# Weighing values before scoring keys in each decode slot of a hybrid decoder step

## The chip, the core and the metric

The kernel runs on one core of one Trainium2 chip. The metric is device time in microseconds (us), the median of several executions; lower is better. One execution is also recorded by the hardware profiler, and all rows below come from that one.

## What is computed

One inference step of a one-layer decoder: a prompt of 16 + 512 tokens and 8 running sequences with 4 new tokens each. The part that matters here is the stick-breaking attention of the running sequences over 4096 cached positions, whose keys and values lie in pages of 128 positions in device memory:

```python
p = x @ w_in                                    # one projection, 53 column blocks of 128
k_past = cache_k[l][page_table].reshape(bs, past, H_ATT, HEAD_DIM)
v_past = cache_v[l][page_table].reshape(bs, past, H_ATT, HEAD_DIM)
z = einsum('bqhd,bkhd->bhqk', q, k) * SB_SCALE + bias
log_keep = where(mask, log_sigmoid(-z), 0.0)
log_pass = cumsum(log_keep, axis=3, reverse=True) - log_keep
a = where(mask, exp(log_sigmoid(z) + log_pass), 0.0)
h_att = einsum('bhqk,bkhd->bqhd', a, v)
```

Beside it stand prompt attention, a short convolution, an mLSTM, an output projection and an MLP. Everything is float32.

## The kernel before

The program has five phases in a row: the input projection together with the decode attention over the cache (`phase_project`), the mixing groups, the output projection, the MLP, and the end. The change is in the first alone.

`phase_project` is laid out by hand in numbered **slots**. Every engine runs its own loop over the same slots k = -16 ... 72, and semaphores tie the loops together. In a slot TensorE multiplies one or two **chunks** of the projection (`chunk`, lines 430 to 432: 16 groups of three matmuls each, about 6.1 us a chunk). Slots 0 to 63 also take one eighth of the cache of one sequence each, in two steps that lie nine slots apart (`LAG = NSTEP + 1 = 9`):

- `scores(k)` (L463) multiplies the transposed keys `kT` of step k with the queries, into `S`. It waits for `kt_done`, VectorE's transpose of the keys (L676). There is one `kT`, so the transpose for step k+1 waits until `scores(k)` is done. GpSimd's gather of the keys for step n (L397, 2 MB, two buffers) waits for the transposes up to step n-2. 
- `weigh(k - 9)` (L478) multiplies the attention weights `aT` of the older step with its values, into `O`. It has two halves. Each half m waits for its own 1 MB of values (`v_in`), which SyncE loads in two transfers (`load_v`, L294) as soon as the value buffer is free; `value_slot` gives three buffers in turn, so the values of half m wait for half m-3 (`av_done`). Hence the second half of a slot gets its values issued after the first half of the slot before, and the first half of a slot after the second half of the slot but one before.

Slots 0 to 8 have `scores` alone, 64 to 72 `weigh` alone, and the 55 slots from 9 to 63 both. Of these 55, 20 have two chunks ("long" slots, some 16 us) and the others one ("short", some 10 us).

SyncE's loop is one queue in order: in slot k it first issues the weight chunks of w_in (`load_w`, L282), each after VectorE's `low` of three chunks earlier (`lo_done`, L669), and then the values that `weigh` of the slot frees. VectorE's loop in slot k does `low` of the chunks of slot k+1, every eighth slot the stick-breaking scan (`stick`), and then the transpose of the keys of step k+1. ScalarE splits the weights (`high`, L547) and empties PSUM (`evac`, L565), in the order first `high` of slot k+1, `evac` of the units that end in slot k, second `high`. At the head of slots 9, 17, ... 65 TensorE turns the weights (`turn`, L491), and one slot later the outputs (`turn_output`, L499).

Of the kernel before, what the change touches and what calls it, by code (L numbers as in the profile page):

```python
# [105 lines left out]
LAG = NSTEP + 1  # L106
# [14 lines left out]
def chunks_of(k):  # L121

    return range(max(0, first_chunk(k)), min(NCHUNK, first_chunk(k + 1)))
# [12 lines left out]
def value_slot(m):  # L136

    return m % VR if m < LAST else (VR, VR + 1, 1, 2, 0)[(m - LAST) % (VR + EXTRA)]
# [7 lines left out]
def value_fill(m):  # L146

    return 1 + sum(value_slot(n) == value_slot(m) for n in range(m))
# [13 lines left out]
def phase_project(nc, dram, keep):  # L162
# [12 lines left out]
    with ExitStack() as ctx:  # L175
# [27 lines left out]
        def value(m, q):  # L203

            slot = value_slot(m)
            return v_nat[:, 2 * slot + q, :] if slot < VR else v_last[:, 2 * (slot - VR) + q, :]
# [196 lines left out]
        def _(pe):  # L403
# [31 lines left out]
            def chunk(n):  # L435

                pe.wait_ge(lo_done, n + 1)
                if gate_chunk(n):
                    g = n - QCHUNK
                    if g == 0:  # L440
                        pe.wait_ge(evac_done, HA - 1)
                    product_of(n, 0, 8, P, 8 * g, g == 0, g == 1).then_inc(chunk_done, 1)
                else:
                    p, part = pair_and_part(n)
                    for j in range(2):
                        if part == 0 and p > 0:
                            pe.wait_ge(evac_done, place(U_GATE) + 1 if 2 * p == HA else place(2 * (p - 1) + j) + 1)
                        last = product_of(n, j, CK, 2 * P, CK * part, part == 0, part == 3)
                        if part == 3 and j == 0:
                            last.then_inc(unit0_done, 1)  # L450
                    last.then_inc(chunk_done, 1)

            def scores(k):
                b, s = divmod(k, NSTEP)
                pe.wait_ge(kt_done, k + 1)
                if s == 0:
                    pe.wait_ge(q_done, b + 1)
                if s % 4 == 0 and b > 0:
                    pe.wait_ge(p_done, 2 * b - 1 + s // 4)
                for g in range(2):  # L460
                    for db in range(4):
                        for j in range(NJ):
                            last = mm(S[32 * j:32 * (j + 1), s // 4, (s % 4) * P:(s % 4 + 1) * P], qd[:, j, g, db, :],  # L463
                                      kT[:, :, 2 * j + g, db, :], start=(g == 0 and db == 0), stop=(g == 1 and db == 3))
                last.then_inc(qk_done, 1)

            def weigh(k):
                b, s = divmod(k, NSTEP)
                if s == 0 and b > 0:
                    pe.wait_ge(o_copied, b)  # L470
                pe.wait_ge(aT_done, 2 * b + 1 + s // 4)
                for half in range(2):
                    m = 2 * k + half
                    pe.wait_ge(v_in[value_slot(m)], 32 * value_fill(m))
                    for q in range(2):
                        quarter = 2 * half + q
                        for j in range(NJ):
                            last = mm(O[32 * j:32 * j + 2 * NQ, 0:2 * HD], aT[:, s, j, quarter, :],  # L478
                                      value(m, q)[:, 2 * HD * j:2 * HD * (j + 1)],
                                      start=(s == 0 and quarter == 0), stop=(s == NSTEP - 1 and quarter == 3))  # L480
                    last.then_inc(av_done, 1)

            def turn(b, half):

                pe.wait_ge(a_done, b + 1)
                if b + half > 0:
                    pe.wait_ge(aT_done, 2 * b + half)
                if b > 1 and half == 0:
                    pe.wait_ge(o_taken, b - 1)
                for s in range(4):  # L490
                    last = tr(X[:, s * P:(s + 1) * P], prob[:, (4 * half + s) * P:(4 * half + s + 1) * P], ident[:, :])  # L491
                last.then_inc(aT_ps, 1)

            def turn_output(b):

                pe.wait_ge(o_copied, b + 1)
                pe.wait_ge(aT_done, min(2 * b + 4, 2 * NB))
                for g in range(2):
                    last = tr(X[:, g * HD:(g + 1) * HD], o_sb[:, g * HD:(g + 1) * HD], ident[:, :])  # L499
                last.then_inc(oT_ps, 1)  # L500

            def turn_gates():

                pe.wait_ge(p_done, 2 * NB)
                pe.wait_ge(gate_dve, 2)
                pe.wait_ge(gate_act, 3)
                for n, row in enumerate((gap, drop)):
                    for t, (t0, r) in enumerate(TT):
                        tr(S[0:r, 0, 64 * n + HM * t:64 * n + HM * (t + 1)], row[:, t0:t0 + r], ident[0:HM, 0:HM])
                tr(S[0:NB, 0, 32:32 + HM], small[:, 64:64 + NB], ident[0:HM, 0:HM]).then_inc(gate_ps, 1)  # L510

            for k in range(-QCHUNK, NSLOT):
                b, s = divmod(k - LAG, NSTEP)
                if b >= 0 and s == 0:
                    turn(b, 0)
                for n in chunks_of(k):
                    chunk(n)
                if b >= 0 and s == 0:
                    turn(b, 1)
                if b > 0 and s == 1:  # L520
                    turn_output(b - 1)
                if 0 <= k < NB * NSTEP:
                    scores(k)
                if b >= 0:
                    weigh(k - LAG)
                if k == TAIL_SLOT + 5:
                    turn_gates()
            turn_output(NB - 1)
# [1890 lines left out]
```

## Time and profile before

| | us |
|---|---|
| median of 3 runs | 2961.32 |
| lowest and highest | 2956.51, 2965.56 |
| the profiled execution's own time | 2960.95 |
| its span, first to last instruction | 2959.2 |
| steps with both parts (slots 9 to 63), about | 213 to 912 |

The rows below are those of the profiled execution. "PE" is TensorE's matmuls and "PEld" its weight loads, which overlap them; DVE is VectorE, ACT ScalarE, POOL GpSimd, SPq SyncE's queue. A busy PE isn't a PE at its peak: matmuls overlap, so what counts is the time from one start to the next.

### The profile page before, as it was taken

How to read it: one execution, taken by the hardware profiler on the slowest of the kernel's cores; microseconds unless marked ns; L12 is line 12 of the kernel's file. 1: busy time of each engine (PE TensorE's matmuls, PEld its weight loads, DVE VectorE, ACT ScalarE, POOL GpSimd, SP SyncE). 2: the span in 40 equal slices, each digit the busy share in tenths (PEclk: the TensorE clock that was granted, in tenths of full speed). 3: DMA queues.
4: the chain of work that ended last, by engine and by line, in shares of the span. 5: the costliest groups of instructions: out<-in, count | busy, mean ns of one | idle time of the engine just before them, and what ended most of it. 6: DMA issues, size and time to landing. Idle time of an engine off the chain costs nothing. (4 is left out here: it accounts for less than half of the span.)

```text
span 2959.2 us, 58893 instructions
## 1 busy us (share of the span) xinstructions
PE 2804.1 (95%) x25775; PEld 2658.9 (90%) x25775; DVE 1886.7 (64%) x2204; ACT 839.4 (28%) x1226; POOL 211.7 (7%) x223
## 2 busy tenths in 40 slices
PE   8999999999999887899899999999999999999995
PEld 8988888888887665899789999999999999999994
DVE  3364555455454685636877777777777777777775
ACT  2222122121122355212533232232232322322321
POOL 2011110111110321001000000000000000000003
PEclk9999999999999899999999999999999999999997
DMA  8789999999999722344222332332323323323222
GB/s 269 263 311 401 400 387 408 405 393 382 397 393 337 249 81 82 93 136 131 63 79 78 94 108 70 110 100 72 115 77 95 108 69 110 100 72 115 78 95 89
DMA packets 340850, 548.62 MB, mean 185 GB/s; under 512 B 20939, under 2 KB 244780, under 8 KB 330018
## 3 DMA queue, kind: packets, MB, share of 16 engines
q1 hardware_dynamic: 319090, 388.38, 39.2%
q0 software_dynamic: 13872, 141.28, 11.9%
q10 hardware_dynamic: 7632, 15.20, 1.3%
q8 instruction: 203, 3.33, 0.4%
q14 instruction: 53, 0.43, 0.0%
HBM read 508.96 MB, written 35.84 MB: 184 GB/s over the span
## 5 line engine op out<-in xcount | busy, mean ns | idle before, releaser
L2116 DVE SCALAR_TENSOR_TENSOR base<-big_G,base 128x544 f32<-128x544 f32 x512 | 370.2, 723 | 244.9 <-PE big_G L1951 244.9
L430 PE MATMUL prj_G<-prj_xh,prj_wh 128*128 128x280 f32 x1696 | 503.9, 297 | 9.2 <-DVE prj_wl L669 9.2
L432 PE MATMUL prj_G<-prj_xh,prj_wl 128*128 128x280 f32 x1696 | 498.5, 294 | 0.0
L431 PE MATMUL prj_G<-prj_xl,prj_wh 128*128 128x280 f32 x1696 | 497.8, 293 | 0.0
L676 DVE STREAM_TRANSPOSE prj_kT<-base 128x4096 f32<-128x4096 f32 x64 | 284.5, 4445 | 325.7 <-PE prj_S L463 322.6
L2028 ACT ACTIVATE wh<-raw 128x1024 fp32r<-128x1024 f32 x227 | 239.3, 1058 | 654.7 <-PE big_G L1951 539.4
L1949 PE MATMUL big_G<-ff_uh,wh 128*128 128x272 f32 x1360 | 392.4, 289 | 3.6 <-DVE base L2116 3.5
L1950 PE MATMUL big_G<-ff_ul,wh 128*128 128x272 f32 x1360 | 393.7, 289 | 0.0
L1951 PE MATMUL big_G<-ff_uh,wl 128*128 128x272 f32 x1360 | 393.6, 289 | 0.0
L430 PEld LDWEIGHTS prj_G<-prj_xh,prj_wh 128*128 128x128 f32 x1696 | 323.0, 190 | 34.1 <-issue 27.3
L2103 DVE TENSOR_TENSOR wl<-raw,wh 128x1024 fp32r<-128x1024 f32 x227 | 277.3, 1221 | 86.0 <-ACT wh L2028 85.7
L432 PEld LDWEIGHTS prj_G<-prj_xh,prj_wl 128*128 128x128 f32 x1696 | 322.6, 190 | 0.0
L431 PEld LDWEIGHTS prj_G<-prj_xl,prj_wh 128*128 128x128 f32 x1696 | 322.6, 190 | 0.0
L1949 PEld LDWEIGHTS big_G<-ff_uh,wh 128*128 128x128 f32 x1360 | 256.5, 189 | 4.0 <-DVE base L2116 4.0
L1950 PEld LDWEIGHTS big_G<-ff_ul,wh 128*128 128x128 f32 x1360 | 257.3, 189 | 0.0
L1951 PEld LDWEIGHTS big_G<-ff_uh,wl 128*128 128x128 f32 x1360 | 256.8, 189 | 0.0
L2028 ACT ACTIVATE big_wh<-raw 128x1024 fp32r<-128x1024 f32 x114 | 120.6, 1058 | 337.2 <-PE big_G L1951 276.0
L669 DVE TENSOR_TENSOR prj_wl<-prj_raw,prj_wh 128x1024 fp32r<-128x1024 f32 x106 | 126.2, 1206 | 133.8 <-ACT prj_wh L547 133.4
L1949 PE MATMUL big_G<-ff_uh,big_wh 128*128 128x272 f32 x688 | 199.4, 290 | 7.4 <-DVE base L2116 3.8
L1949 PE MATMUL big_G<-big_xh,wh 128*128 128x272 f32 x688 | 201.3, 293 | 1.0 <-ACT base L2031 1.0
L1950 PE MATMUL big_G<-ff_ul,big_wh 128*128 128x272 f32 x688 | 199.8, 290 | 0.0
L1951 PE MATMUL big_G<-ff_uh,big_wl 128*128 128x272 f32 x688 | 199.8, 290 | 0.0
(414 smaller groups left out, 6013.8 us busy)
## 6 DMA issues: line engine op xcount, KB each, us to landing
prj_v_nat<-in_cache_v SPq DMA_DIRECT2D x242, 512.0 KB, 7.6
raw<-in_w_down SPq DMA_DIRECT2D x128, 512.0 KB, 4.4
raw<-in_w_up SPq DMA_DIRECT2D x120, 512.0 KB, 4.4
prj_raw<-in_w_in SPq DMA_DIRECT2D x106, 512.0 KB, 12.8
raw<-in_w_out SPq DMA_DIRECT2D x16, 1024.0 KB, 7.3
prj_scratch<-prj_stage ACTq DMA_DIRECT2D x53, 280.0 KB, 8.9
out_xr<-x_scratch SPq DMA_DIRECT2D x16, 544.0 KB, 3.7
base<-in_cache_v SPq DMA_DIRECT2D x14, 512.0 KB, 6.8
```

The costliest lines, as they stand in the source:

```text
L430: mm(out, w_hi[:, k, m], xh[:, k0 + k, cols], start=(first and k == 0), stop=False)
L431: mm(out, w_hi[:, k, m], xl[:, k0 + k, cols], start=False, stop=False)
L432: last = mm(out, w_lo[:, k, m], xh[:, k0 + k, cols], start=False, stop=(end and k == nk - 1))
L669: V.tensor_tensor(wl[n % WH][:, :, :], raw[n % RAW][:, :, :], wh[n % WH][:, :, :].bitcast(F32), ALU.subtract).then_inc(lo_done, 1)
L676: V.transpose(flat(kT[:, :, :, :, :].rearrange("p r h b i -> p r (h b i)")), flat(k_nat[k % 2][:, :, :]))\
L1949: mm(out, w_hi, x_hi, start=start, stop=False)
L1950: mm(out, w_hi, x_lo, start=False, stop=False)
L1951: return mm(out, w_lo, x_hi, start=False, stop=stop)
L2028: A(ring_h[slot % RING], Q[q], ACT.Copy).then_inc(hi_done, 1)
L2103: V.tensor_tensor(ring_l[slot % RING], Q[q], ring_h[slot % RING].bitcast(F32), ALU.subtract).then_inc(lo_done, 1)
L2116: V.scalar_tensor_tensor(out, G[2 + t % 2][:, :, 0:HALF_M], 1.0 / ALPHA, out, ALU.mult, ALU.add).then_inc(y_done, 1)
```

## The change

In TensorE's loop two calls change places. The loops of all other engines stay word for word as they were.

```diff
                 if b > 0 and s == 1:
                     turn_output(b - 1)
+                if b >= 0:
+                    weigh(k - LAG)
                 if 0 <= k < NB * NSTEP:
                     scores(k)
-                if b >= 0:
-                    weigh(k - LAG)
                 if k == TAIL_SLOT + 5:
                     turn_gates()
```

TensorE's instructions around slot 31, where L463 is `scores`, L478 `weigh` and L430 to L432 a chunk; a float32 matmul of L463 or L478 counts as two in the trace. Before, the scores stand between the chunk and the values:

```order
L432 MATMUL prj_G<-prj_xh,prj_wl 128x280
L463 MATMUL prj_S<-prj_kT,prj_qd 32x128 [waits prj_kt_done]
L463 MATMUL prj_S<-prj_kT,prj_qd 32x128 x31
L478 MATMUL prj_O<-prj_v_nat,base 8x256 [waits prj_v_in2,prj_aT_done]
L478 MATMUL prj_O<-prj_v_nat,base 8x256 x7
L478 MATMUL prj_O<-prj_v_nat,base 8x256 [waits prj_v_in0]
L478 MATMUL prj_O<-prj_v_nat,base 8x256 x7
L430 MATMUL prj_G<-prj_xh,prj_wh 128x280 [waits prj_lo_done]
```

In the changed kernel, the same place:

```order
L432 MATMUL prj_G<-prj_xh,prj_wl 128x280
L478 MATMUL prj_O<-prj_v_nat,base 8x256 [waits prj_v_in2,prj_aT_done]
L478 MATMUL prj_O<-prj_v_nat,base 8x256 x7
L478 MATMUL prj_O<-prj_v_nat,base 8x256 [waits prj_v_in0]
L478 MATMUL prj_O<-prj_v_nat,base 8x256 x7
L463 MATMUL prj_S<-prj_kT,prj_qd 32x128 [waits prj_kt_done]
L463 MATMUL prj_S<-prj_kT,prj_qd 32x128 x31
L430 MATMUL prj_G<-prj_xh,prj_wh 128x280 [waits prj_lo_done]
```

The values moved ahead of the scores with all their waits; the chunk's neighbour behind is now the scores. SyncE's order around the same slot is the same in both kernels: a weight chunk, then the two transfers of a second half, then (after the next wait) those of a first half.

```order
L282 DMA prj_raw2<-in_w_in 128x4x256 [waits prj_lo_done]
L84 TENSOR_LOAD prj_pages [waits prj_av_done]
L84 ISA x2
L294 ISA
L294 DMA prj_v_nat<-in_cache_v 128x1024
```

Nothing moved there, but the first of the two waits follows VectorE's work behind the scores, and the second follows the values.

## Rows read from the trace of the kernel before

**Rows 1.** The page: busy time and share of each engine, and total traffic.
```profile
span 2959.2 us, 58893 instructions
PE 2804.1 (95%) x25775; PEld 2658.9 (90%) x25775; DVE 1886.7 (64%) x2204; ACT 839.4 (28%) x1226; POOL 211.7 (7%) x223
```

**Rows 2.** Busy time by stretch: before, through and behind the 55 slots, then three short ones.
```profile
core 0: us, PE busy (x) PEld busy (x) DVE busy (x) ACT busy (x) POOL busy (x), PEclk, DMA share, GB/s
213.00:910.00 697.00, 676.57 (x8798) 604.28 (x8797) 357.03 (x196) 144.35 (x241) 77.77 (x52) 0.99 1.00 393
...
910.00:985.00 75.00, 66.59 (x723) 52.94 (x722) 20.16 (x52) 19.56 (x28) 3.65 (x13) 0.95 0.86 319
...
500.00:600.00 100.00, 99.02 (x1301) 88.77 (x1303) 52.41 (x31) 21.35 (x35) 11.95 (x8) 1.00 1.02 403
...
412.00:416.00 4.00, 4.00 (x54) 2.93 (x47) 3.75 (x1) 1.92 (x3) 0.00 (x0) 1.00 0.76 254
694.00:698.00 4.00, 4.00 (x72) 2.93 (x65) 3.13 (x1) 0.00 (x0) 0.00 (x0) 1.00 0.45 157
```

**Rows 3.** Waits of TensorE from 130 to 1000 us: total, times, longest.
```profile
PEld prj_O L478 <- DMA prj_v_nat<-in_cache_v: 30.1, 20, 3.1
PEld prj_G L430 <- DVE prj_wl L669: 6.7, 3, 5.9
...
PE prj_O L478 <- DMA prj_v_nat<-in_cache_v: 20.3, 17, 2.6
```

**Rows 4.** TensorE's weight loads around slot 31's scores and values: start, length, count.
```profile
495.53 0.19 PEld L432 LDWEIGHTS prj_G<-prj_xh,prj_wl 128*128 128x128 f32 x1
495.87 1.69 PEld L463 LDWEIGHTS prj_S<-prj_kT,prj_qd 128*32 128x32 f32 x64 [0.16 <-issue]
497.54 1.51 PEld L478 LDWEIGHTS prj_O<-prj_v_nat,base 128*8 128x8 f32 x32
499.48 0.19 PEld L430 LDWEIGHTS prj_G<-prj_xh,prj_wh 128*128 128x128 f32 x1 [0.43 <-issue]
```

**Rows 5.** The same around slot 4, which has scores and no values.
```profile
165.20 0.19 PEld L432 LDWEIGHTS prj_G<-prj_xh,prj_wl 128*128 128x128 f32 x1
165.55 1.69 PEld L463 LDWEIGHTS prj_S<-prj_kT,prj_qd 128*32 128x32 f32 x64 [0.16 <-issue]
167.43 0.19 PEld L430 LDWEIGHTS prj_G<-prj_xh,prj_wh 128*128 128x128 f32 x1 [0.20 <-issue]
```

**Rows 6.** The same at slot 64, which has values and no scores.
```profile
926.03 0.19 PEld L432 LDWEIGHTS prj_G<-prj_xh,prj_wl 128*128 128x128 f32 x1
926.37 0.33 PEld L478 LDWEIGHTS prj_O<-prj_v_nat,base 128*8 128x8 f32 x12 [0.16 <-issue]
```

**Rows 7.** TensorE's matmuls of a long slot (30), without the chunks.
```profile
483.77 1.95 PE L463 MATMUL prj_S<-prj_kT,prj_qd 128*32 128x128 f32 x64
485.55 1.05 PE L478 MATMUL prj_O<-prj_v_nat,base 128*8 128x256 f32 x16
488.52 1.05 PE L478 MATMUL prj_O<-prj_v_nat,base 128*8 128x256 f32 x16 [1.93 <-DMA prj_v_nat<-in_cache_v]
```

**Rows 8.** The short slot before it (29): matmuls, then VectorE, GpSimd, SyncE's queue.
```profile
467.63 1.96 PE L463 MATMUL prj_S<-prj_kT,prj_qd 128*32 128x128 f32 x64
469.40 1.91 PE L478 MATMUL prj_O<-prj_v_nat,base 128*8 128x256 f32 x32
...
459.75 4.45 DVE L676 STREAM_TRANSPOSE prj_kT<-base 128x4096 f32<-128x4096 f32 x1 [4.78 <-PE prj_S L463]
464.12 2.32 DVE L669 TENSOR_TENSOR prj_wl<-prj_raw,prj_wh 128x1024 fp32r<-128x1024 f32 x2
469.73 4.45 DVE L676 STREAM_TRANSPOSE prj_kT<-base 128x4096 f32<-128x4096 f32 x1 [3.29 <-PE prj_S L463]
...
464.46 1.65 POOL L397 DMA_INDIRECT base<-in_cache_k,prj_key_rows  x1 [8.68 <-DVE prj_kT L676]
474.44 0.94 POOL L397 DMA_INDIRECT base<-in_cache_k,prj_key_rows  x1 [8.33 <-DVE prj_kT L676]
...
465.33 1.53 SPq L282 DMA_DIRECT2D prj_raw<-in_w_in  x2
471.22 5.90 SPq L294 DMA_DIRECT2D prj_v_nat<-in_cache_v  x4
```

**Rows 9.** Landing times: value transfers of 462 to 478 us, then all key gathers from 210 us.
```profile
DMA to landing us min/median/max: 7.1/13.6/14.2
...
DMA to landing us min/median/max: 10.8/12.5/13.6
```

**Rows 10.** Waits of VectorE's key transpose, from 210 to 910 us.
```profile
L676 DVE STREAM_TRANSPOSE prj_kT<-base x54: 4435/4446/4447, 215.3 to 902.3; 128x4096 f32<-128x4096 f32 x54
...
  PE prj_S L463: 307.0, 48
```

**Rows 11.** Slot 21, short, in whose chunk a unit ends: ScalarE, VectorE, SyncE's queue.
```profile
363.68 0.64 ACT L565 ACTIVATE prj_stage<-prj_G 128x560 f32<-128x560 f32 x1 [2.44 <-PE prj_G L432]
...
365.16 1.05 ACT L547 ACTIVATE prj_wh<-prj_raw 128x1024 fp32r<-128x1024 f32 x1
...
365.30 1.23 DVE L669 TENSOR_TENSOR prj_wl<-prj_raw,prj_wh 128x1024 fp32r<-128x1024 f32 x1 [4.06 <-ACT prj_wh L547]
366.44 4.43 DVE L676 STREAM_TRANSPOSE prj_kT<-base 128x4096 f32<-128x4096 f32 x1
...
362.30 4.64 SPq L282 DMA_DIRECT2D prj_raw<-in_w_in  x2
367.70 5.25 SPq L294 DMA_DIRECT2D prj_v_nat<-in_cache_v  x4
```

**Rows 12.** The values of slot 22, the long slot behind it.
```profile
381.49 1.05 PE L478 MATMUL prj_O<-prj_v_nat,base 128*8 128x256 f32 x16
385.11 1.75 PE L478 MATMUL prj_O<-prj_v_nat,base 128*8 128x256 f32 x16 [2.58 <-DMA prj_v_nat<-in_cache_v]
```

**Rows 13.** SyncE's queue: what it waited for from 213 to 910 us.
```profile
SPq L84 <- PE prj_O L478: 334.1, 57, 12.7
SPq L282 <- DVE prj_wl L669: 45.9, 35, 5.9
```

## The prediction

> **What bounds the kernel now.** I read the page first: TensorE is busy for 95% of the span [rows 1], so time can only come from TensorE's path, its gaps or what feeds it. The change touches 55 slots of one stage, so next comes the table by stretch. From 213 to 910 us PE is busy for 676.6 of 697 us, and at the same time the DMA engines' share is 1.00 at 393 GB/s [rows 2]. Two resources are full at once. The list of waits says how they meet: nearly all that TensorE waits for in this stage are values from the cache, 30.1 us in 20 waits on the load side, the longest 3.1 us, and 20.3 us in 17 seen at the matmuls (the same stalls, seen twice) [rows 3]. That is the second half of `weigh`, as in slot 30, where the scores start at 483.77, the first half at 485.55 and the second only at 488.52 [rows 7]. Its transfers were issued from 471.22 on [rows 8], and took a median of 13.6 us to land there [rows 9]. They were not late by a microsecond of queueing in front of them but stood in a backlog. So in the stalled slots the stage runs at the speed of the DMAs, and in others at TensorE's: around 412 us and 694 us DMA share falls to 0.76 and 0.45 while PE is busy for all 4 us [rows 2].
>
> **What the change moves.** No instruction is added or removed; other engines keep their order. Per period (one slot) both orders hold one scores block, one weigh block and the chunks. So the distance from one `scores` to the next, and from one `weigh` to the next, is the same sum as before. Only the phase between them shifts: weigh comes earlier by a scores block, 497.54 - 495.87 = 1.67 us, and scores later by a weigh block, 499.48 - 497.54 = 1.94 us, less the change of neighbour below [rows 4]. Relative to each other they move by about 3.5 us.
>
> **Term 1: changes of neighbour on TensorE.** Start to start on the weight loads, the order before costs at its joints: last chunk load to scores 495.87 - 495.53 = 0.34; last scores load to first weigh load 0.09 (the scores' 64 loads begin 1.67 before it, at a pitch of 1.58/63 us); last weigh load to the chunk: the 32 loads end at 499.05, the last began 0.09 earlier, so 499.48 - 498.96 = 0.52 [rows 4]. Sum 0.95 us. The new order: chunk to weigh 926.37 - 926.03 = 0.34 [rows 6]; weigh to scores, which the trace never shows; scores to chunk, from slot 4, where the last scores load began at 165.55 + 1.69 - 0.11 = 167.13: 0.30 [rows 5]. Sum 0.64 us plus the unknown. The unknown from the nearest rows: 0.05, the pitch inside weigh (1.51 us for 32), if it costs nothing; 0.09, its mirror image, scores to weigh; 0.52, if it is as dear as weigh to a chunk. That gives a saving of 0.26, 0.22 or a loss of 0.21 us a slot. I take it near 0.09, since scores and weigh both use quarters of the array's columns (128*32 and 128*8 in the rows) and the mirror join is the nearest row. But weigh's longer matmuls (0.4 against 0.27 us) drain somewhere, and I allow 0.1 us for that: saving 0.1 to 0.2, say 0.16 us a slot, times 55 = 8.8 us of TensorE's time (ends: -14 and +12).
>
> The Trainium skill, TensorEngine Tiling (Array Packing), Key Properties, says that changing the tiling mode drains the engine and changing the tile does not. By that rule weigh to scores is a change of tile alone, and the sum would stand at its cheap end, about -12 us. This trace agrees as far as its joints go (0.09 within the mode, 0.30 to 0.52 out of it), but has no row of weigh to scores.
>
> **Term 2: how much of that reaches the end.** A TensorE that gets to a second half sooner than its values land hands the time back. Every group of eight slots has a stall (20 in 55 slots), so what is saved is returned at the next one, unless the DMAs go faster too. What they can still give is their dips. At the rate of the best shown 100 us, 403 GB/s against 393, the 697 us would be 17 us shorter [rows 2]; the two dips shown are worth (1 - 0.76) x 4 + (1 - 0.45) x 4 = 3 us, and they are not the only ones. I take a third of term 1: **-3 us**.
>
> **Term 3: the landing of values.** Issue follows the weigh before, the need comes one period later; both shift alike, so the window stays. Two things in it change. For it: the key gather, 2 MB that take 12.5 us [rows 9] and so are in flight nearly always, now starts about 3.5 us later seen from weigh (before, at 464.46 and 474.44 around a weigh at 469.40 [rows 8]); at the moment when slot 30's second half needs its values, less of the next gather has been moved, and more of the values. Against it: weight chunks come closer before the values on the same queue. Before, `load_w` stood at 465.33, well ahead of the values at 471.22 [rows 8]; now it follows a transpose that starts later and is issued about 2 us before. Same queue order, same bytes, a queue that is never empty at that point: I cost both at nothing in sum, with the ends in the rivals.
>
> **Term 4: covers that shrink.** The keys: the transpose waits for scores in 48 of 54 cases, 307 us in all, and for no gather in this stretch [rows 10], and the gather's window (transpose to transpose but one) does not shrink except that a stall of weigh now lies before the scores of its slot instead of behind. The cover of `scores` itself grows, since a weigh now lies between the chunk and it. The weights: `low` of the next slot stands behind the transpose, so it moves 1.9 us later against the chunk that needs it, while TensorE's waits for it are 6.7 us in the whole stage, 5.9 of them once [rows 3], at a place behind the last scores. Cost nothing. `turn` at slots 17, 25, ... now follows scores and loses 1.9 us of cover for the scan; these slots come behind long ones, whose 12 us chunk pair covers the scan, and no wait of theirs is in the list. Cost nothing.
>
> **Sum.** -3 us. The profiled execution had 2960.95 (span 2959.2 and 1.75 around it), 0.4 below the median of 2961.32. So 2960.95 - 3 = 2958.
>
> **Rivals.**
>
> *A, values land in time (faster).* If the gather's later start lets the values through, the stalls shrink and the DMA's dips fill. For it: the stalls are short, 1.5 us on average, against a shift of 3.5 us x 160 GB/s or so (2 MB in 12.5 us) = 0.56 MB, which at 393 GB/s is 1.4 us. Against it: share 1.00 over 697 us. It is limited by the 17 us above; I price it at two thirds, -12 us: 2949.
>
> *B, SyncE is held in front of the values (slower).* Where a short slot before a long one ends a unit, ScalarE's second `high` waits for the chunk's end and `evac`: in slot 21 the `evac` starts at 363.68, `high` ends at 366.21, `low` at about 367.4, and the values go out at 367.70, just after [rows 11]. Six such slots exist (15, 18, 21, 47, 50, 53). With weigh 1.7 us earlier the values would be wanted at about 366.0 and still go out at 367.7 or later, while their deadline is 1.7 us sooner. Slot 22's second half already waits 2.58 us [rows 12], so the wait grows there: 6 x 1.7 = 10 us; and a stall now also holds back the scores, the transpose and the key gather of the slot, where before it held only the next chunk. With 0.3 us for each of the other 14 long slots that is +14: 2975. It decides if the queue drains between its weight chunk and its values; if the backlog lasts, the issue time does not matter. SyncE waits 45.9 us for `low` now against 334.1 for weigh [rows 13], so it is mostly on time today.
>
> *C, weigh to scores drains the array.* 0.52 instead of 0.09: +0.21 x 55 = +12 us, 2973; some of it falls into stalls, but most slots have none.
>
> *D, nothing at all moves*: 2961, inside the forecast's range.
>
> The Trainium skill, DMA: Bandwidth & Descriptors, Queues, rings and completion order, says that each DMA engine takes turns between the queues packet by packet. By that rule a gather that starts later leaves more of the turns to the values first and fewer afterwards, which is rival A within a slot and nothing over a period; a sum by it alone would be A's or D's. No row here shows turns.
>
> **How the numbers follow.** A measurement of this kernel tells 0.3%, 8.9 us, from no change: faster is below 2952.4, slower above 2970.2. Forecast with D: 0.60. A: 0.18, faster. B: 0.15 and C: 0.07, slower. So faster 0.18, same 0.60, slower 0.22. The forecast's own range is 2951 to 2968; with 8 in 10 to hold, it must reach to most of A and into B and C: 2945 to 2974.
>
> **What would show it.** In the profile of the changed kernel: the joints weigh to scores and scores to chunk at 0.09 to 0.2 and 0.30 us (term 1); waits of `weigh` for values between 25 and 40 us on the load side, DMA share still 1.00 (term 2). A shows as waits for values under 20 us and a stage shorter by 10. B shows as more than 40 us of such waits, with SyncE waiting for `low` for clearly more than 45.9 us. C shows in the joint itself. The forecast is wrong if scores come to wait for the transpose, or the transpose for a gather: then a cover that I called free was the bound.

## The result

| | before | after |
|---|---|---|
| median, us | 2965.05 (18 runs) | 2979.85 (18 runs) |
| lowest and highest | 2952.38, 2975.71 | 2973.13, 2995.83 |
| profiled execution, span | 2959.2 | 2976.3 |

The ratio after to before is 1.0051, with a 95% interval of 1.0037 to 1.0066. The change makes the kernel about 15 us slower. I had forecast 2958 us, -3, in a range of 2945 to 2974; the measured time lies above the range and on the other side of before.

### The profile after

The page and the table by stretch. Columns as in [rows 1] and [rows 2].

```profile
span 2976.3 us, 58893 instructions
PE 2805.9 (94%) x25775; PEld 2658.8 (89%) x25775; DVE 1886.2 (63%) x2204; ACT 839.4 (28%) x1226; POOL 212.2 (7%) x223
```

```profile
213.00:932.00 719.00, 682.63 (x8872) 608.91 (x8868) 357.31 (x196) 143.30 (x241) 78.27 (x52) 0.98 0.98 384
```

The same work is in it (PE busy for 2805.9 us against 2804.1 [rows 1]). The 55 slots took 720 us instead of 700, first instruction of slot 9 to the last of slot 63; the rest gave 3 us back. The DMAs moved 384 GB/s over them instead of 393 [rows 2], at a share of 0.98 against 1.00: they moved less in the same time and were idle a little more often.

TensorE's waits from 130 to 1000 us, which answer to [rows 3]:

```profile
PEld prj_O L478 <- DMA prj_v_nat<-in_cache_v: 47.5, 24, 7.8
...
PEld prj_G L430 <- DVE prj_wl L669: 7.3, 3, 6.5
```

Waits for values rose from 30.1 to 47.5 us. The waits for weight chunks did not change, and no wait for the transposed keys has appeared. To see where, I took the wait of the second half slot by slot: TensorE's idle time on the load side just before it, as that list counts it (from 0.15 us up). The sums for slots 9 to 63:

| wait of the second half, us | before | after |
|---|---|---|
| long slots 16, 19, 22, 48, 51, 54 ("the six") | 12.5 | 21.1 |
| the other 14 long slots | 12.1 | 1.9 |
| slot 13 | 0.0 | 7.8 |
| the other short slots | 5.2 | 16.0 |
| all | 29.9 | 46.8 |

The other long slots gained 10.2 us, everything else lost about 27. In the six the wait is nearly a constant, 3.4 to 3.7 us. The longest, slot 13, shows a second cost. These are its matmuls, and three stretches around them (columns as in [rows 2], of which the last three are granted clock, DMA share, GB/s):

```profile
259.14 1.05 PE L478 MATMUL prj_O<-prj_v_nat,base 128*8 128x256 f32 x16
267.48 1.90 PE L478 MATMUL prj_O<-prj_v_nat,base 128*8 128x256 f32 x16 [7.29 <-DMA prj_v_nat<-in_cache_v]
```

```profile
251.00:259.00 8.00, 8.00 (x116) 7.78 (x107) 6.04 (x3) 1.36 (x2) 1.33 (x1) 1.00 1.01 389
259.00:262.00 3.00, 1.19 (x18) 0.34 (x16) 0.64 (x1) 1.06 (x1) 0.32 (x1) 1.00 1.04 418
262.00:272.00 10.00, 4.53 (x72) 3.29 (x76) 0.00 (x0) 0.00 (x0) 0.00 (x0) 0.50 1.03 410
```

TensorE had been idle since about 260 us when the granted clock fell to 0.50, its lower level of 1.2 GHz, and it stayed there to 272, although the values had come at 267.5. Summed over the 55 slots, the clock's record has 10.2 us at half clock before and 23.9 after. At half the clock at most half of that time is lost, where TensorE has work: 5 and 12 us. So waits +17 and clock up to +7 cover the 20 us of the stage.

### The profile page after: what moved, and what is told of

Read it like the earlier page. It is cut to its first block and busy times, and to the rows that moved or that the text cites. A ratio compares the mean times of both kernels' runs of the same rounds, so it can differ in the third digit from the quotient of the medians.

```text
span 2976.3 us, 58893 instructions
## 1 busy us (share of the span) xinstructions
PE 2805.9 (94%) x25775; PEld 2658.8 (89%) x25775; DVE 1886.2 (63%) x2204; ACT 839.4 (28%) x1226; POOL 212.2 (7%) x223
## 5 line engine op out<-in xcount | busy, mean ns | idle before, releaser
L430 PE MATMUL prj_G<-prj_xh,prj_wh 128*128 128x280 f32 x1696 | 503.3, 297 | 10.1 <-DVE prj_wl L669 9.6
L432 PE MATMUL prj_G<-prj_xh,prj_wl 128*128 128x280 f32 x1696 | 497.3, 293 | 0.0
L430 PEld LDWEIGHTS prj_G<-prj_xh,prj_wh 128*128 128x128 f32 x1696 | 321.9, 190 | 23.6 <-issue 16.3
L432 PEld LDWEIGHTS prj_G<-prj_xh,prj_wl 128*128 128x128 f32 x1696 | 321.7, 190 | 0.0
## 6 DMA issues: line engine op xcount, KB each, us to landing
prj_raw<-in_w_in SPq DMA_DIRECT2D x106, 512.0 KB, 10.8
```

Source lines behind the costliest of these rows:

```text
L430: mm(out, w_hi[:, k, m], xh[:, k0 + k, cols], start=(first and k == 0), stop=False)
L432: last = mm(out, w_lo[:, k, m], xh[:, k0 + k, cols], start=False, stop=(end and k == nk - 1))
```

## The experiments

Every group of runs stood beside its own runs of the kernel before, on the same chip, whose median was 2963 to 2972 us. I therefore compare ratios to before. Theory Q of the expectations is rival B of the prediction. The waits are those of the list of waits for values, load side, from 213 to 910 us, in one profiled execution each.

| kernel | ratio to before, 95% interval | waits, us | of these, the six |
|---|---|---|---|
| before | 1 | 29.9 | 12.5 |
| after, first result | 1.0051 (1.0037 to 1.0066) | 46.8 | 21.1 |
| x1 after, again | 1.0047 (1.0032 to 1.0062) | 47.1 | 21.7 |
| x2 after, scores first in the six | 0.9985 (0.9972 to 0.9999) | 28.6 | 6.3 |
| x3 before, weigh first in the six | 1.0086 (1.0064 to 1.0107) | 45.2 | 24.1 |
| x4 after, both splits first | 1.0046 (1.0029 to 1.0063) | 41.5 | 21.4 |
| x6 before, half the values | 0.9861 (0.9838 to 0.9884) | 0.2 | 0.0 |
| x7 after, half the values | 0.9914 (0.9891 to 0.9936) | 13.1 | 10.0 |
| x10 after, six gathers held | 0.9987 (0.9972 to 1.0003) | 43.1 | 0.4 |
| x12 before, all gathers later | 0.9951 (0.9931 to 0.9972) | 13.4 | 5.0 |
| x14 after, all gathers later | 1.0049 (1.0027 to 1.0070) | 44.7 | 4.9 |
| y1 after, seven store pairs late | 0.9981 (0.9962 to 0.9999) | 26.4 | 0.0 |
| z1 before, seven store pairs late | 0.9982 (0.9963 to 1.0001) | 33.2 | 6.7 |
| y4 before, all stores late | 1.0052 (1.0036 to 1.0068) | 35.7 | 7.1 |
| y3 before, gathers and all stores late | 0.9994 (0.9974 to 1.0014) | 30.7 | 0.0 |
| z2 before, gathers and seven pairs late | 0.9950 (0.9929 to 0.9970) | 5.1 | 0.5 |
| z3 before, all gathers later, again | 0.9968 (0.9948 to 0.9987) | 8.9 | 3.4 |

(The expectations counted the waits of slots by a looser sum, which holds up to 0.2 us in a slot that does not wait and came out larger: 12.7 and 21.8 us where the first two rows have 12.5 and 21.1.)

### Where it costs: x1, x2, x3

x1 is the changed kernel again. x2 puts the scores first in the six long slots alone, x3 puts weigh first there alone:

```diff
+                first = b >= 0 and (k not in (16, 19, 22, 48, 51, 54))   # x2; "k in" for x3
+                if first:
+                    weigh(k - LAG)
                 if 0 <= k < NB * NSTEP:
                     scores(k)
-                if b >= 0:
+                if b >= 0 and not first:
                     weigh(k - LAG)
```

> The changed kernel again, for a second profile. Theory Q (SyncE is held by the weight chunk in front of the values in the six short slots 15, 18, 21, 47, 50, 53, so the long slots behind them wait): about 15 us slower than before, second-half waits of 3 to 4 us again in slots 16, 19, 22, 48, 51 and 54, about 9 us more in these six than before. Rival O (one odd event: the 7.8 us wait of slot 13 at 259 us and the clock stretch behind it, together about 10 us, is what made it slower): the event is absent here and the kernel is within 8 us of before.

> The changed kernel, but in the six long slots 16, 19, 22, 48, 51 and 54 scores go first as before; the values of these slots are then wanted 1.9 us later and issued at the same time. Theory Q: the six waits shrink by about 1.7 us each, 8 to 10 us in all, so 5 to 8 us slower than before. Rival C (all 55 slots pay for the new order on TensorE or on the queue, evenly): 49/55 of the loss stays, 13 us slower than before.

> The kernel before, but with weigh first in the same six long slots alone. Only the deadline of the values moves (1.7 us sooner), not their issue. Theory Q: the six waits grow by up to 1.7 us each, 6 to 10 us slower than before. Rival C: 6/55 of 15 us, under 2 us.

x1 repeated the loss and its pattern: the six at 3.4 to 3.9 us each, and slot 13 at 7.9. So slot 13 was no accident of one run, though its size varies: x2 is the same program up to slot 15, and there it waited 3.3 us. x2 gave back all of the loss, not the 8 to 10 us that I had expected: it was 0.15% faster than before. x3 lost 0.86%, more than the whole change, with six slots of 55. The even rival is out. These are the stretches 213 to 910 us of x2 and x3:

```profile
213.00:910.00 697.00, 677.54 (x8908) 606.75 (x8901) 358.87 (x198) 144.80 (x242) 76.81 (x52) 1.00 1.01 398
```

```profile
213.00:910.00 697.00, 660.08 (x8454) 586.59 (x8452) 343.91 (x190) 139.88 (x236) 78.26 (x52) 0.97 0.97 380
```

The third number from the end is the granted clock: 1.00 in x2, 0.97 in x3, whose clock record has 0 and 41 us at the lower level in the 55 slots. The six waits, 11.6 us more than before, are somewhat under half of x3's loss of 25 us. Slot 45 waits 6.7 us instead of 2.9, and the lower clock can have taken up to 15 us more.

### Not SyncE's hold: x4

```diff
-                for n in ahead[0:1]:
+                for n in ahead:
                     high(n)
...
                 for u in ending(k):
                     evac(u)
-                for n in ahead[1:]:
-                    high(n)
```

> The changed kernel, with ScalarE's second split of the weights moved ahead of the emptying of PSUM, so that the second weight chunk no longer waits for the end of the slot's own chunk. Theory Q: the values of the six slots go out about 1.9 us after weigh starts again instead of 3.9, the six waits fall from 3.4 to about 1.7 us each, 8 to 10 us faster than the changed kernel. Rival D (the DMAs are the bound, the issue time of a transfer does not matter): same as the changed kernel within 3 us, with the same waits.

The hold was there, and x4 removed it in the six: their values go out 1.8 to 2.0 us after the weigh of the slot before starts, instead of 3.9 to 4.2. But the time did not move (1.0046), and the six waits stayed at 3.3 to 3.9 us. Slot 19 shows why. For each kernel follow the weight chunk or chunks (L282) and the values (L294) on SyncE's queue, the stores (L572) on ScalarE's, the next key gather (L397), the landing times of the values issued there, and the two halves of weigh. Before:

```profile
326.20 0.33 ACTq L572 DMA_DIRECT2D prj_scratch<-prj_stage  x1
...
330.13 3.54 SPq L294 DMA_DIRECT2D prj_v_nat<-in_cache_v  x3
...
333.57 1.81 POOL L397 DMA_INDIRECT base<-in_cache_k,prj_key_rows  x1 [9.12 <-DVE prj_kT L676]
...
DMA to landing us min/median/max: 11.9/13.4/15.0
...
346.25 1.05 PE L478 MATMUL prj_O<-prj_v_nat,base 128*8 128x256 f32 x16 [1.08 <-DMA prj_v_nat<-in_cache_v]
```

After:

```profile
335.34 0.33 ACTq L572 DMA_DIRECT2D prj_scratch<-prj_stage  x1
335.36 1.91 PE L478 MATMUL prj_O<-prj_v_nat,base 128*8 128x256 f32 x32
...
339.26 4.46 SPq L294 DMA_DIRECT2D prj_v_nat<-in_cache_v  x4
...
343.87 1.81 POOL L397 DMA_INDIRECT base<-in_cache_k,prj_key_rows  x1 [8.54 <-DVE prj_kT L676]
...
DMA to landing us min/median/max: 9.8/15.0/15.2
...
355.67 1.05 PE L478 MATMUL prj_O<-prj_v_nat,base 128*8 128x256 f32 x16 [3.15 <-DMA prj_v_nat<-in_cache_v]
```

x4:

```profile
325.86 0.99 ACTq L572 DMA_DIRECT2D prj_scratch<-prj_stage  x2
325.96 1.91 PE L478 MATMUL prj_O<-prj_v_nat,base 128*8 128x256 f32 x32
...
327.79 6.37 SPq L294 DMA_DIRECT2D prj_v_nat<-in_cache_v  x4
...
DMA to landing us min/median/max: 11.9/14.7/17.5
...
346.40 1.05 PE L478 MATMUL prj_O<-prj_v_nat,base 128*8 128x256 f32 x16 [3.27 <-DMA prj_v_nat<-in_cache_v]
```

In the kernel after, the values go out 3.90 us after weigh starts (339.26 - 335.36), in x4 1.83 us. The second transfer of the half lands 15.2 us after its issue in the one and 17.5 in the other. Issuing it 2 us sooner made it fly 2 us longer. Something else fixes its arrival: in both kernels the last transfer landed within 1.1 us of the next key gather's landing (356.5 after, 347.4 in x4), and in the kernel before too (346.2 against 346.7). Over the six, the last transfer lands within 1.6 us of that gather in the changed kernel, and within 1.5 us in the kernel before, except in slot 22 (385.1 against 382.0).

### Is it the gather, or the bytes? x10, x12, x6, x7

x10 holds the gather that starts in each of the six until that slot's values have landed. x12 makes every gather from slot 9 on wait for the slot's first chunk, in the order before:

```diff
                 else:
                     po.wait_ge(kt_done, n - 1)
+                if n - 2 in (16, 19, 22, 48, 51, 54):
+                    po.wait_ge(v_in[value_slot(2 * (n - 2 - LAG) + 1)], 32 * value_fill(2 * (n - 2 - LAG) + 1))
```

```diff
                 else:
                     po.wait_ge(kt_done, n - 1)
+                if n - 2 >= LAG:
+                    po.wait_ge(chunk_done, first_chunk(n - 2) + 1)
```

> The changed kernel; the key gather that starts in each of the six long slots 16, 19, 22, 48, 51 and 54 waits until the values of that slot's second half have landed. Theory G (with weigh first the gather starts about 3.5 us later against the values, the last value transfer shares the DMAs with it to its end and lands with it, so the wait of the second half ends when the gather ends; the stalls over 3 us also bring low clock stretches): the six waits fall from 3.6 us to under 1 us each, the kernel is 12 to 18 us faster than the changed one, about as fast as the one before. Rival T (the DMAs are simply full, whoever comes first): the same bytes take the same time, the waits move to the short slots or to the keys, within 4 us of the changed kernel.

> The kernel before, in its own order on TensorE; each key gather from slot 9 on also waits for the first chunk of its slot, so that it starts about 3.3 us later in every slot and nothing else moves. Theory G: 10 to 20 us slower than before, with waits in the six slots over 3 us, as in the changed kernel. Rival P (what costs is the values' deadline or TensorE's order, not the gather's phase): within 4 us of before.

x10 took the six waits from 21.1 to 0.4 us and was about 0.6% faster than the changed kernel, as theory G had said. Its profiled execution does not show that gain: it is the slowest of its runs and has 43.1 us of waits, 28.4 of them in short slots other than 13 (16.0 after) and 7.3 in the other long ones (1.9), which is the sign that rival T named. x12 came out on the other side of G: 0.5% faster than before instead of slower, and 0.3% in the repeat z3. So "a gather that starts later is bad" was wrong. What the two share is the distance between the values' last issue and the next gather's start. In the six of the kernel before it was 0.7 to 2.3 us. In x12 it was 5.7 to 6.2, and the waits of all long slots but four vanished (22 and 48 kept under 1 us, 54 and 59 some 4). In the changed kernel it was 5.6 us or more in the other long slots (62 has no gather behind it), which is where the change gained 10.2 us, and 3.2 to 4.5 in the six. Distance alone does not decide, though: in x4 the six had 5.4 to 6.5 us of it and waited as in the changed kernel.

The later gather is not free. The list of waits, from 213 to 910 us, has more short idle stretches of TensorE that end with no releaser, before and in x12 (its lines are numbered 2 higher):

```profile
PEld prj_S L463 <- issue: 8.6, 54, 0.2
...
PEld prj_O L478 <- issue: 0.2, 1, 0.2
```

```profile
PEld prj_S L465 <- issue: 17.0, 75, 0.5
...
PEld prj_O L480 <- issue: 5.9, 14, 0.5
```

The 55 slots of x12's profiled execution, the slowest of eight, took 701 us like those of before, with 16.5 us less of waits for values; z3's took 696. What causes these gaps was not tested.

x6 and x7 leave out the second of the two transfers of every half, in the order before and after. TensorE weighs the first transfer's rows twice, so its work is the same and the decode attention is not computed rightly.

```diff
-                pe.wait_ge(v_in[value_slot(m)], 32 * value_fill(m))
+                pe.wait_ge(v_in[value_slot(m)], 16 * value_fill(m))
...
-                value(m, q)[:, 2 * HD * j:2 * HD * (j + 1)],
+                value(m, 0)[:, 2 * HD * j:2 * HD * (j + 1)],
...
-                for q in range(2):
+                for q in range(1):
```

> The kernel before, with only the first of the two value transfers of each half loaded (TensorE weighs its rows twice, so that its work is the same and the attention output is not). With 1 MB less in each slot no value should be late: waits for values under 2 us in all, and a stage about 35 to 45 us shorter.

> The changed kernel with the same half of the value transfers left out. What remains between it and the same edit of the kernel before is the price of the order on TensorE alone. Theory G, from the joints of the two profiles (3.81 against 3.83 us a slot without chunks): within 2 us of each other. Rival C (the order itself costs TensorE or VectorE time): 10 us or more between them.

I had expected no waits and a tie. The order still cost 16.6 us between the two medians (0.9861 and 0.9914, four runs each). By the number that is rival C's, but the profile shows no dearer TensorE: x7 waits 13.1 us for values, x6 0.2. 10.0 us of it stand in three of the six (16, 22 and 54). And this is with DMAs that are not full on average. The stretches 213 to 850 us of x6, then of x7:

```profile
213.00:850.00 637.00, 637.00 (x8413) 573.42 (x8404) 340.49 (x188) 139.75 (x236) 76.64 (x51) 1.00 0.89 329
```

```profile
213.00:850.00 637.00, 626.97 (x8184) 564.63 (x8180) 332.45 (x185) 134.38 (x231) 74.96 (x50) 0.99 0.86 323
```

The third number from the end is the granted clock, the second the DMA share. A mean of 0.86 hides bursts, though. These are two stretches of x7, ahead of the values of slot 16 and while they are in flight:

```profile
281.00:289.00 8.00, 8.00 (x131) 6.82 (x130) 4.79 (x4) 2.59 (x4) 1.65 (x1) 1.00 0.51 169
289.00:303.00 14.00, 13.09 (x111) 12.22 (x109) 10.12 (x10) 5.31 (x18) 0.94 (x1) 1.00 1.01 401
```

The share is 0.51 and then 1.01; over the flights that slots 22 and 54 wait for it is 0.98 and 0.95. So the engines are full while the late transfer is in flight, and have room over the stage. That ends the reading on which my forecast stood: the wait is one transfer's lateness in a local jam, not the stage's throughput.

### The stores: y1, z1, y4, y3, x14

What the six share is that they are long slots and that two projection units end in the short slot ahead of them, where ScalarE issues two stores of 280 KB just before the values. Slot 13 has such a pair ahead of it too. So have slots 10, 42 and 45, short ones, which wait 1.0, 2.0 and 2.7 us after and 0.6, 1.3 and 2.9 before: the pair alone does not make a long wait. y1 issues these seven pairs one slot later, in the changed kernel; z1 does the same in the kernel before, y4 and y3 with all stores of slots 9 to 62 (y3 on top of x12), z2 with the seven on top of x12.

```diff
+        def LATE(k):
+            return k in (12, 15, 18, 21, 47, 50, 53)      # y4, y3: LAG <= k < TAIL_SLOT - 1
...
                 for u in ending(k):
-                    store(u)
+                    if not LATE(k):
+                        store(u)
+                for u in ending(k - 1):
+                    if LATE(k - 1):
+                        ac.wait_ge(chunk_done, min(NCHUNK, first_chunk(k) + 1))
+                        store(u)
```

> The changed kernel; the stores of the projection units that end in slots 12, 15, 18, 21, 47, 50 and 53 (two of 280 KB each time) are issued one slot later, behind that slot's first chunk. Theory S (in these slots the two stores go out just ahead of the values of the next slot's second half; with weigh first these values follow them by 1 us instead of 3, miss the time before the next key gather and land with the gather, 15 to 17 us after their issue; that is what slots 13, 16, 19, 22, 48, 51 and 54 wait for): the seven waits fall from 3.6 (13: 8) to under 1 us, the kernel is 12 to 18 us faster than the changed one. Rival W (it is the two weight chunks or the gather's phase, and stores are too small to matter): the waits stay over 3 us, within 4 us of the changed kernel.

> The kernel before with the same seven pairs of stores one slot later as in y1, the control for it. Theory S (the loss of the new order is the meeting of values and stores in these seven slots): before has less to gain there, its six waits are 12.7 us against 21.8, so it gets 3 to 12 us faster than before, and the two orders then differ by less than 8 us instead of 15. Rival V (late stores help any order by the same amount): about 20 us faster than before, and the order still costs 15.

y1 gives the whole loss back and more: 0.9981, against 1.0051 and 1.0047 for the changed kernel. The six waits fell from 21.1 us to none, slot 13 from 7.8 to 1.7. Slot 19 of y1, to be read beside the three above (its lines are numbered 3 higher):

```profile
329.07 4.06 SPq L297 DMA_DIRECT2D prj_v_nat<-in_cache_v  x4
...
333.77 1.81 POOL L400 DMA_INDIRECT base<-in_cache_k,prj_key_rows  x1 [8.66 <-DVE prj_kT L684]
...
335.33 0.90 ACTq L575 DMA_DIRECT2D prj_scratch<-prj_stage  x2
...
DMA to landing us min/median/max: 8.1/9.0/9.2
...
341.39 1.91 PE L481 MATMUL prj_O<-prj_v_nat,base 128*8 128x256 f32 x32
```

The first of the values goes out at the same distance from the gather as after, 4.7 us against 4.6. Without the stores ahead of them they fly 9.2 us at most instead of 15.2, and both halves run in one piece. The edit moved nothing else of the values' issue: in the six they follow the weigh of the slot before by 3.9 to 4.2 us in both kernels. z1 is the control: the kernel before ends at 0.9982 with the same edit, a gain of 0.18% that is at the edge of the noise (its six go from 12.5 to 6.7 us). With the seven pairs out of the way the two orders take the same time within about 0.3%, where the change had cost 0.5%. These two runs tie the loss of the change to the seven meetings.

> The changed kernel, each key gather from slot 9 on also waits for the first chunk of its slot, about 1.6 us later. Theory L (a value transfer that is issued long enough before the next gather lands before it; in the kernel before the distance was 2 us, with the later gather 6 us, here it becomes 7): waits of the seven slots fall, 5 to 15 us faster than the changed kernel. Rival U (what helped the kernel before was not the distance): same as the changed kernel within 4 us, or slower because the keys come late.

x14 tests the distance to the gather in the changed kernel. The six waits did fall, to 4.9 us, but those of the short slots, 13 among them, rose from 23.8 to 39.8, and the time stayed at 1.0049. Theory L was right on the slots that it named and wrong on the sum.

> The kernel before, with all stores of slots 9 to 62 issued one slot later. Theory S: the waits of slots 16, 19, 22, 48, 51 and 54, 12.7 us in all, fall to that of the other long slots or below, 3 to 8 us faster than before. Rival W: within 3 us.

> The kernel before with both the later gather and the later stores. If the two act on different waits, this is the fastest: 2 to 5 us faster than the later gather alone, that is 17 to 20 us faster than before. If the later gather took all waits already, the same as it.

y4 missed: the six waits fell to 7.1 us as expected, but the kernel got 0.5% slower, with waits of 6.2 and 5.9 us in slots 29 and 37, which had none before. A store that is moved meets other values. y3 lost most of x12's gain in the same way. So late stores are no gain as such; it matters which values they meet.

> The kernel before with the later gather and the seven stores late. The later gather left 17.7 us of waits, of which 5.9 in the six slots; if the stores are what is behind these, 2 to 6 us faster than the later gather alone. If delaying stores disturbs other slots, as it did when all were delayed, no gain or a loss.

> The kernel before with the later gather alone, once more beside the other two: 10 to 15 us faster than before if the first result holds, with waits for values below 20 us.

z3 confirms the later gather (0.9968, waits of 8.9 us). z2 adds the seven late pairs: waits for values 5.1 us in all, the fewest of the kernels that do the whole work, and 0.9950. Its interval overlaps those of x12 and z3, so I claim no gain over the later gather alone, but each of the three beats both kernels of this case.

## Why the prediction was wrong

**What bounds the kernel.** I read a DMA share of 1.00 beside the waits for values as "the stage runs at the speed of the DMAs". That reading of a mean misled me: with a backlog that never ends the issue and the order of single transfers would not matter, and so I priced term 3 at nothing. x7 waits in three of the same slots at a mean share of 0.86, and at 0.95 to 1.01 while the late transfer is in flight. A stage's share tells that the engines have something to do, not which transfer must be late.

**Term 1, neighbours on TensorE: mis-sized.** I took 0.16 us saved a slot. These are the joints after, to be read as [rows 4]:

```profile
507.48 0.19 PEld L432 LDWEIGHTS prj_G<-prj_xh,prj_wl 128*128 128x128 f32 x1
507.82 1.41 PEld L478 LDWEIGHTS prj_O<-prj_v_nat,base 128*8 128x8 f32 x32 [0.16 <-issue]
509.34 1.87 PEld L463 LDWEIGHTS prj_S<-prj_kT,prj_qd 128*32 128x32 f32 x64
511.41 0.19 PEld L430 LDWEIGHTS prj_G<-prj_xh,prj_wh 128*128 128x128 f32 x1 [0.20 <-issue]
```

Chunk to weigh is 0.34 and scores to chunk 0.30, as taken from [rows 5, 6]. Weigh to scores is 509.34 - 509.14 = 0.20 where I had 0.09, and the scores' own loads now take 1.87 us instead of 1.69. From the last chunk load to the next one it is 3.93 us, against 3.95 in [rows 4]: 0.02 us a slot, 1 us in all instead of 8.8. Most other slots without a wait give the same two numbers within 0.01 us. Rival C's 0.52 is out. The Trainium skill, TensorEngine Tiling (Array Packing), Key Properties, has a change of mode drain the engine and not a change of tile, and this trace agrees as far as 0.20 lies below the 0.30 to 0.52 of a change of mode. The 12 us that I worked out beside it did not come.

**Term 2** had nothing left to pass on.

**Term 3, the landing of values: the step that failed.** I set the two effects of the shift against each other and wrote nothing for the sum, where the runs showed +17 us of waits and up to 7 of clock. Both effects were there. Rival A's is the gain of 10.2 us in the other long slots, where the values now lead the gather by some 6 us. Against it stand +8.6 in the six, +7.8 in slot 13, +10.8 in the other short slots, and the lower clock. I never looked at the stores of ScalarE's queue, which are not in the change but go out at the end of the chunk, just where the change moved the weigh to.

**Term 4, the covers,** held: no wait for keys or transposes appeared, those for weight chunks stayed at 7 us.

**Rival B** came nearest, and I gave it 0.15. Its place was right, and its price there: 1.7 us in each of six slots, 10 us, where the trace has 8.6. That its total of 14 us stands beside the 15 measured is luck: it had 4 us more for the other long slots, which gained 10.2, and nothing for slot 13, the short slots and the clock. Its mechanism was wrong. It also misread a row: `low` ended at 365.30 + 1.23 = 366.53 [rows 11], not at about 367.4. SyncE's wait for `low` did rise, from 45.9 us [rows 13] to 222.6, but x4 shows that an earlier issue brings no earlier landing. What fits the runs is that it matters whether the values get through before the next gather takes its share. With two stores ahead of them they don't, and they land with the gather, at a time that no longer depends on their issue, while weigh wants them 1.7 us sooner. That the stores are the load that tips it is shown by y1 against the changed kernel. That the chain runs through the gather is supported by x10's median and waits of the six and by the landing times, and how the three share the engines is not shown.

**The range** left out two sizes: slot 13, a short slot whose wait went from nothing to 7.8 and 7.9 us in the two profiles of the changed kernel (3.0 to 3.4 in x2, x4 and x14), and the clock.

**What stays open.** The short slots' further loss of 10.8 us I only argue: their values go out 3 us behind the start of a gather now, where before the gather in flight was some 7 us old (slot 29: 472.38 behind 469.10 after, 461.24 behind 454.13 before). I did not test it alone. x2 has the same 16.0 us in these slots and is no slower than before, so this loss is about paid for by the gain of the other long slots. Nor did I separate the clock's part from the waits that it follows.

## What to carry to other kernels

When the list of waits names a transfer, look up what was issued on every queue in the microseconds around it, and where it lands against its neighbours, before calling the DMAs the bound. Leaving out half of the bytes tells lateness from throughput in one run; read the DMA share then in the microseconds of the wait, and not only over the stage. In a pipeline laid out by hand, a swap that leaves every period alone still moves phases, and the few slots where a rare event (here the stores of a finished unit) meets the moved step can decide the sign; list them by slot, and price those apart.

## What the runs showed of the hardware

- The second value transfer of a half, 512 KB, issued 3.2 to 6.5 us ahead of a 2 MB gather and with two stores of 280 KB ahead of it, lands within 1.2 us of the gather: after 14.9 to 17.9 us, in slots 16, 19 and 22 of the changed kernel and of x4. Without the stores, and 2.9 to 4.7 us ahead of the gather, it takes 8.2 to 12.5 us in the six slots of y1. The page of the changed kernel lists SyncE's queue (q1) with many small packets, 1.2 KB on average, and the gather's (q0) with few large ones, 10 KB (packets, MB, share of the engines):

```profile
q1 hardware_dynamic: 319090, 388.38, 39.4%
q0 software_dynamic: 13872, 141.28, 11.8%
```

  The Trainium skill, DMA: Bandwidth & Descriptors, Queues, rings and completion order, says that the engines take turns by packet. If its packets are those of the page of the profile, the gather would get more bytes a turn by that rule, which would fit, but no run here changes packet sizes.
- Around the end of some waits of TensorE, stretches of 3.4 to 10.2 us at a granted clock of 0.50 begin (262 to 272 us in the changed kernel). In the kernel before, the three of the stage follow an idle time of the matmuls of 2.2 to 2.6 us. Not each wait has one: of the six of 3.4 to 3.7 us in the changed kernel two have. x3, with the largest waits in the six (24.1 us), has 41 us of it, x2 none.
- Weigh to scores, two uses of a quarter of the array's columns, costs 0.20 us from load to load one way round and 0.09 the other.
